# Two transformer blocks on one core: the last MLP's up product with seven block products per pair of feature tiles

## The reference

```python
h = _rmsnorm_2(x, mlp_norm_w[layer])
x = x + jnp.square(jax.nn.relu(h @ w_up[layer])) @ w_down[layer]
```

## Time and profile before

| | us |
|---|---|
| median of 3 runs | 3357.95 |
| lowest and highest | 3356.92, 3360.74 |
| span of the profiled execution | 3358.0 |
| its own busy time: PE, DVE, POOL, ACT | 3155.6, 1537.2, 1206.1, 816.2 |
| output product 2538 to 2643, last MLP 2643 to 3358 | 105, 715 |

### The profile page before, as it was taken

How to read it: one execution, slowest core, us unless ns; L and a number is a source line. 1 busy time by engine, 2 the same in 40 slices (tenths; PEclk the granted TensorE clock), 3 DMA queues, 4 the chain that set the end, 5 groups by cost and what they waited for, 6 DMA issues and landing times.

```text
span 3358.0 us, 34815 instructions
## 1 busy us (share of the span) xinstructions
PE 3155.6 (94%) x13555; PEld 2467.7 (73%) x13566; DVE 1537.2 (46%) x2220; ACT 816.2 (24%) x1186; POOL 1206.1 (36%) x567
## 2 busy tenths in 40 slices
PE   7999998999878799999999799889998999999999
PEld 5787775678656588888887477568666788888887
DVE  3799956553643621221122621255884532232236
ACT  3312215511224301000001332245774100000000
POOL 2254342334722244344333133173002344444443
PEclk9899999999989999999999899999999999999999
DMA  2022310034110011111111122442421111111111
GB/s 103 26 88 100 139 44 7 1 138 150 63 38 19 25 49 46 50 50 44 50 50 44 40 75 100 123 150 69 106 76 72 44 45 50 50 50 44 50 50 75
DMA packets 69272, 217.54 MB, mean 65 GB/s; under 512 B 7468, under 2 KB 18900, under 8 KB 68408
## 3 DMA queue, kind: packets, MB, share of 16 engines
q1 hardware_dynamic: 40832, 145.51, 14.0%
q10 hardware_dynamic: 28344, 70.74, 5.7%
HBM read 175.31 MB, written 40.65 MB: 64 GB/s over the span
## 4 chain that ended last, share of the span: by engine, by line
PE 87%; DVE 6%; ACT 4%; issue 1%; POOL 1%; ACTq 0%; DMA 0%; POOLq 0%; DVEq 0%
PE ps L519 25%; PE ps L521 25%; PE ps L520 25%; PE ps L557 3%; PE ps L720 2%; DVE y L1672 1%; PE ps L1036 1%; PE ps L1024 1%; DVE x L1673 1%; PE ps L710 1%; PE ps L1009 1%; POOL w_lo L419 1%; PE ps L1010 1%; DVE acc L1649 0%; POOL w_hi L416 0%
## 5 line engine op out<-in xcount | busy, mean ns | idle before, releaser
L416 POOL TENSOR_TENSOR w_hi<-w_raw,zero 128x1024 fp32r<-128x1024 f32 x210 | 407.5, 1940 | 1808.9 <-PE ps L521 1801.9
L519 PE MATMUL ps<-normed_hi,w_hi 128*128 128x512 f32 x1488 | 588.8, 396 | 34.7 <-DVE normed_lo L1657 18.2
L520 PE MATMUL ps<-normed_lo,w_hi 128*128 128x512 f32 x1488 | 583.7, 392 | 0.0
L521 PE MATMUL ps<-normed_hi,w_lo 128*128 128x512 f32 x1488 | 583.6, 392 | 0.0
L419 POOL TENSOR_TENSOR w_lo<-w_raw,w_hi 128x1024 fp32r<-128x1024 f32 x210 | 564.4, 2687 | 16.5
L519 PEld LDWEIGHTS ps<-normed_hi,w_hi 128*128 128x128 f32 x1488 | 282.5, 190 | 100.3 <-issue 28.6
L519 PE MATMUL ps<-hidden_hi,w_hi 128*128 128x512 f32 x864 | 336.9, 390 | 2.8 <-DVE hidden_lo L1888 2.8
L521 PE MATMUL ps<-hidden_hi,w_lo 128*128 128x512 f32 x864 | 336.8, 390 | 0.0
L520 PE MATMUL ps<-hidden_lo,w_hi 128*128 128x512 f32 x864 | 336.6, 390 | 0.0
L520 PEld LDWEIGHTS ps<-normed_lo,w_hi 128*128 128x128 f32 x1488 | 282.5, 190 | 60.8 <-issue 2.2
L521 PEld LDWEIGHTS ps<-normed_hi,w_lo 128*128 128x128 f32 x1488 | 282.2, 190 | 59.4
(11 more groups left out here) (360 smaller groups left out, 5179.9 us busy)
## 6 DMA issues: line engine op xcount, KB each, us to landing
w_raw<-weights_dram SPq DMA_DIRECT2D x228, 512.0 KB, 3.7
gates_scratch<-tmp ACTq DMA_DIRECT2D x24, 512.0 KB, 2.7
gated<-gates_scratch ACTq DMA_DIRECT2D x24, 512.0 KB, 5.4
head_part<-diff_qk_scratch SPq DMA_DIRECT2D x48, 256.0 KB, 6.4
x_in<-x_dram ACTq DMA_DIRECT2D x4, 1024.0 KB, 11.1
x<-x_dram ACTq DMA_DIRECT2D x1, 4096.0 KB, 13.9
diff_qk_scratch<-d_hi ACTq DMA_DIRECT2D x8, 512.0 KB, 2.7
diff_qk_scratch<-d_out ACTq DMA_DIRECT2D x8, 512.0 KB, 2.7
```

The source lines that it names most:

```text
L416: nc.gpsimd.tensor_tensor(w_hi[s][:], raw[s][:], zero[:, 0:1].broadcast_to([P, 1024]), ALU.add).then_inc(w_rounded, 1)
L519: nc.tensor.matmul(out, sh, mh, start=start, stop=False)
L520: nc.tensor.matmul(out, sh, ml, start=False, stop=False)
L521: return nc.tensor.matmul(out, sl, mh, start=False, stop=stop)
```

## The change

The 4096 features of the last MLP are taken in PAIRS = 16 pairs of tiles. The up product of a pair is seen as a 2 x 2 by 2 x 2 block product: the left side is weights (2 feature tiles by 2 halves of 4 input tiles), the right side x (2 halves of the input tiles by 2 halves of the tokens). A scheme of Strassen's kind (seven products, with sums ahead and behind) takes the place of eight block products. One block product is 4 x 3 = 12 matmuls into one PSUM bank.

- The sums of the right side (t1 to t4, minus_b22) are made once, and split (`right`, 7 pairs of 4 x 512 columns), by ACT and DVE; they fill the place of x, normed and hidden. So x goes to DRAM (`x_kept`) tile by tile from ACT's queue, is scaled in place, and comes back as `x_back` in the last pair from SP's queue.
- The sums of the left side are made by POOL per pair from four 128 x 512 parts. The high part is now rounded by ACT (`left_hi`), the remainder made by POOL (`left_rest`), with 4 buffers of 512 columns, used in turn. Per pair there are 11 of these: products 0 to 4, four for down, products 9 and 10. A22 is loaded a second time.
- Behind the products, ACT copies the first, and DVE forms the four quarters of the pair in 7 steps (`u_read`, `v_read`, `c12_read`, `c22_read` with two, `c11_read`, `c21_read`; they count in `post_done`); ACT takes relu, square and rounding (`hidden_part`), DVE the remainder (`hidden_rest`).
- The order on PE for pair c: products 0 to 4, the down product of pair c - 1 (8 tiles of 12 matmuls, two PSUM slots in turn), products 9 and 10. After the loop the down product of the last pair follows.
- Down results are added to `y_2`, in the place of x; the clearing of it waits for all of the right side. For output tiles 4 to 7 y_2 times acc goes to x_back one pair early, and the last pair's result is then multiplied from PSUM.

The diff, cut to its core ("..." where lines are left out; of the removed lines only the loop's; the DVE steps, `hidden_part` and the packing of the weights are told above):

```diff
-PRE_ORDER = ("mix_pre", "mem_pre", "ffn_pre", "attn_2", "q_a", "kv_a", "mlp_2")
+PRE_ORDER = ("mix_pre", "mem_pre", "ffn_pre", "attn_2", "q_a", "kv_a")
...
+PAIRS = FF2_TILES // 2
+LEFT = 11
+A11, A21, A22, A12, DOWN = 0, 1, 2, 3, 4
+A22_AGAIN = DOWN
+RAW_OF_LEFT = (A11, A22, A11, A11, A21, DOWN, DOWN + 1, DOWN + 2, DOWN + 3, A12, A22_AGAIN)
+BY_FIRST, BY_DOWN, BY_PLAIN = range(5), range(5, 9), (9, 10)
...
+        left = [(at(f"left_hi{i}", SPLIT + 4 * KB * i, [P, HALF], F32R),
+                 at(f"left_lo{i}", SPLIT + 4 * KB * i + 2 * KB, [P, HALF], F32R)) for i in range(4)]
+        part_at = [RAW + 2 * KB * i for i in range(4)] + [late_at + 2 * KB * i for i in range(4)]
+        part_in = [at(f"part_in{i}", o, [P, HALF]) for i, o in enumerate(part_at)]
+        right = {name: pair("right_" + name, o, [P, 4, HALF]) for name, o in (
+            ("b11", BR), ("t1", BR + 16 * KB), ("t2", BR + 32 * KB), ("minus_b22", BR + 48 * KB),
+            ("t3", AR), ("b21", AR + 16 * KB), ("t4", AR + 32 * KB))}
...
+        y_2 = at("y_2", XR, [P, KT, S])
+        x_back = at("x_back", BR, [P, KT, S])
...
+            def load_left(c, before, last=False):
+                first = isinstance(c, int) and c == 1
+                if not last:
+                    for i, used in ((A22, 2), (A11, 3), (A21, 4)):
+                        sp.wait_ge(w_split, before(used))
+                        load_part(i, c)
+                if first:
+                    sp.wait_ge(right_lo, right_0 + 28)
+                else:
+                    sp.wait_ge(w_split, before(5))
+                    load_again(c - 1)
+                if last:
+                    sp.wait_ge(w_used, left_at(PAIRS - 1, 1))
+                    for k in range(KT):
+                        sp.dma_start(x_back[:, k, :], t["x_kept"][k]).then_inc(x_back_in, 16)
+                for i in range(1, 4):
+                    sp.wait_ge(w_split, before(5 + i))
+                    load_part(DOWN + i, c - 1)
+                if not last:
+                    sp.wait_ge(w_split, before(9))
+                    load_part(A12, c)
+                sp.wait_ge(w_split, before(10))
+                load_part(DOWN, c - 1)
...
+            def left_rest(c, i):
+                hi, lo = left[i % 4]
+                pool.wait_ge(w_rounded, left_at(c, i))
+                tt(lo[:], part_in[RAW_OF_LEFT[i]][:], hi[:].bitcast(F32), ALU.subtract).then_inc(w_split, 1)
+            def split_pair(c, down=True):
+                pool.wait_ge(pair_landed, 48 * c + landed_0 + 48)
+                add_part(A22, A21, 1)
+                pool.wait_ge(left_summed, 4 * c + summed_0 + 1)
+                add_part(A21, A11, 2)
+                left_rest(c, 0)
+                pool.wait_ge(left_summed, 4 * c + summed_0 + 2)
+                pool.wait_ge(w_split, left_at(c, 0))
+                add_part(A11, A22, 3)
+                left_rest(c, 1)
+                left_rest(c, 2)
+                pool.wait_ge(late_landed, 16 * c + landed_0 + 16)
+                pool.wait_ge(w_split, left_at(c, 2))
+                add_part(A11, A12, 4)
+                for i in (3, 4, 5, 6, 7, 8, 9, 10) if down else (3, 4, 9, 10):
+                    left_rest(c, i)
...
+            def left_product(c, i, bank, name, ready=None):
+                hi, lo = left[i % 4]
+                pe.wait_ge(w_split, left_at(c, i))
+                for k in range(4):
+                    if ready:
+                        pe.wait_ge(right_lo, right_0 + ready[k])
+                    last = product(ps[:, bank, :], (hi[:, k * P:k * P + P], lo[:, k * P:k * P + P]),
+                                   tuple(v[:, k, :] for v in right[name]), k == 0, k == 3)
+                last.then_inc(w_used, 1)
+            def pair_first(c):
+                first = isinstance(c, int) and c == 0
+                pe.wait_ge(*((x_added, 3 * KT + 5) if first else (post_done, 7 * c + post_0 - 2)))
+                left_product(c, 0, 0, "b11", (7,) * 4 if first else None)
+                pe.wait_ge(*((x_added, 3 * KT + 6) if first else (post_done, 7 * c + post_0 - 1)))
+                left_product(c, 1, 2, "t1", (8,) * 4 if first else None)
+                if not first:
+                    pe.wait_ge(post_done, 7 * c + post_0)
+                left_product(c, 2, 1, "t2", (14, 14, 14, 16) if first else None)
+                if first:
+                    pe.wait_ge(x_added, 4 * KT)
+                left_product(c, 3, 7, "minus_b22", (15,) * 4 if first else None)
+                pe.wait_ge(first_copied, c + copied_0 + 1)
+                left_product(c, 4, 0, "t3", range(17, 21) if first else None)
...
+                pe.wait_ge(post_done, 7 * c + post_0 + 2)
+                left_product(c, 9, 2, "b21", range(21, 25) if first else None)
+                left_product(c, 10, 1, "t4", range(25, 29) if first else None)
...
+                pe.wait_ge(u_lo, 4 * c)
+                for m in range(KT):
+                    hi, lo = left[(5 + m // 2) % 4]
+                    if m % 2 == 0:
+                        pe.wait_ge(w_split, left_at(c, 5 + m // 2))
+                    pe.wait_ge(u_added, 8 * c + m - 1)
+                    for k in range(2):
+                        b = (m % 2 * 2 + k) * P
+                        for n in range(0, S, HALF):
+                            last = product(down_slot(m)[:, n:n + HALF], (hi[:, b:b + P], lo[:, b:b + P]),
+                                           tuple(v[:, k, n:n + HALF] for v in hidden_2), k == 0, k == 1)
+                    last.then_inc(w_used if m % 2 else first_half, 1)
...
-            mlp_chunk(0, 2)
-            with pe.Fori(1, FF2_TILES // CHUNK) as c:
-                mlp_chunk(c)
+            over_features(wide(2), acc, ones[:]).then_inc(n_sum, 1)
+            pair_last(0)
+            pe.wait_ge(n_rs, 10)
+            with pe.Fori(1, PAIRS) as c:
+                pair_first(c)
+                down_2(c)
+                pair_last(c)
+            down_2(PAIRS)
...
+            for k in range(KT - 1):
                 act.wait_ge(x_added, 3 * KT + k + 1)
+                act.dma_start(t["x_kept"][k], x[:, k, :]).then_inc(x_kept, 16)
                 post_square(3, k, x[:, k, :])
+                act.wait_ge(x_kept, kept_0 + 16 * k + 16)
+                act.wait_ge(n_post_sq, 3 * KT + k + 1)
+                nc.scalar.activation(x[:, k, :], x[:, k, :], ACT.Copy, scale=col("mlp_2", k)).then_inc(right_scaled, 1)
+                act.wait_ge(right_scaled, scaled_0 + k + 1)
+                if k < 4:
+                    right_round("b11", k, x[:, k, n1])
+                    act.wait_ge(right_formed, right_0 + k + 1)
+                    right_round("t1", k, t1_plain[:, k, :])
+                else:
+                    right_round("minus_b22", k - 4, x[:, k, n2], -1.0)
+                    act.wait_ge(right_formed, right_0 + k + 1)
+                    right_round("t2", k - 4, x[:, k - 4, n1])
+            left_hi(0, 0)
+            left_hi(0, 1)
+            left_hi(0, 2)
+            act.wait_ge(x_added, 4 * KT)
+            act.dma_start(t["x_kept"][KT - 1], x[:, KT - 1, :]).then_inc(x_kept, 16)
+            nc.scalar.activation(last_scaled[:], x[:, KT - 1, :], ACT.Copy, scale=col("mlp_2", KT - 1)).then_inc(right_scaled, 1)
+            act.wait_ge(right_scaled, scaled_0 + KT)
+            right_round("minus_b22", 3, last_scaled[:, n2], -1.0)
+            act.wait_ge(right_formed, right_0 + KT)
+            right_round("t2", 3, x[:, 3, n1])
...
+            copy_first(0)
+            left_hi(0, 3)
+            left_hi(0, 4)
+            for j in range(4):
+                right_round("t3", j, x[:, j, n2])
+            left_hi(0, 9)
+            post_square(3, KT - 1, x[:, KT - 1, :])
+            for j in range(4):
+                right_round("b21", j, x[:, 4 + j, n1] if j < 3 else last_scaled[:, n1])
+            left_hi(0, 10)
+            for j in range(4):
+                act.wait_ge(right_formed, right_0 + KT + j + 1)
+                right_round("t4", j, t4_plain[:, j, :])
...
+            with act.Fori(1, PAIRS) as c:
+                left_hi(c, 0)
+                hidden_c12(c - 1)
+                left_hi(c, 1)
+                hidden_c11(c - 1)
+                left_hi(c, 2)
+                hidden_c22(c - 1)
+                hidden_c21(c - 1)
+                copy_first(c)
+                for i in range(3, LEFT):
+                    left_hi(c, i)
+            hidden_c12(PAIRS - 1)
+            left_hi(PAIRS, 5)
+            hidden_c11(PAIRS - 1)
+            left_hi(PAIRS, 6)
+            hidden_c22(PAIRS - 1)
+            left_hi(PAIRS, 7)
+            hidden_c21(PAIRS - 1)
+            left_hi(PAIRS, 8)
...
+            def right_sums(j, second):
+                dve.wait_ge(right_scaled, scaled_0 + 5 + j)
+                dve.wait_ge(right_lo, right_0 + 8)
+                step(tt(x[:, j, n2], x[:, j, n2], second[:, n2], ALU.subtract))
```

(95 more changed lines are left out.)

215 lines of the change are left out of this document (139 added, 76 removed).

## The result

| | before | after |
|---|---|---|
| median, us | 3358.1 | 3335.0 |
| lowest and highest | 3356.9, 3360.7 | 3332.2, 3342.1 |
| span of the profiled execution | 3358.0 | 3340.3 (its time 3342.1) |

Both medians are of four runs. The ratio is 0.9935 (95% interval 0.9923 to 0.9948): 23 us, or 0.65%, faster, where 26 were predicted. The forecast's own case came in; 3335.0 lies 3.0 above its 3332.0.

What follows compares the result with a forecast made beforehand. TensorE matmuls were taken to bound the kernel. MLP start 2642.65, pair 0 and total 20.4 + 5.5, 15 pairs 612.3, clear 8, wait 10, last down 30, store 3.1: 3332 us after rounding, range 3318 to 3348.

Steps and rivals of the forecast that it cites:

- Removed matmuls, 43.5 us: Last MLP: 84 up matmuls per feature pair, not 96; 192 fewer at 0.2267 us save 43.5 us.
- Steady loop 0: Loop over pairs: added ACT, DVE and POOL work stays covered, costing 0 beyond matmuls; left 3 has 1.1 us to spare.
- Pair 0, 5.5 us: MLP entry: DVE's queue of sums and remainders makes product 10 end late, costing 5.5 us (4 to 12).
- Clear, 8 us: Pair 1: DVE's 6.9 us clear of y_2 ahead of c11_read delays products 1 to 3, costing 8 us (5 to 12).
- Wait before the last down product, 10 us: After the last pair's product 10, PE waits for hidden, made serially by ACT and DVE: 10 us (6 to 13).
- Last down product 30 us: Last down product to its last sum: DVE's three operations on tiles 0 to 3 hold up PE; 30 us.
- The round trip, 0: Return of x as x_back: its 4 MB load is covered, costing 0, at most 5 us.
- 1 (cheaper transitions): Transitions: DVE at its fast rows, no low clock, end wait 7, giving 3319 us; chance 0.12.
- 2: Loop: left 3 late in every pair by 0.3 to 1 us at full clock, 3336 to 3347 us; chance 0.15.
- 3: Loop: left 3's chain over 2 us late and the clock falls in each pair, 3388 us, slower; chance 0.06.
- 4, a clock that falls at the joins alone: Joins between 12-matmul groups: one clock fall a pair of 1.7 to 2.8 us, 3359 to 3377 us; chance 0.04.
- 5: Whole MLP: the change does not do what it says, matmuls stay at 3072, 3375 us; chance 0.01.

Runs made afterwards that it cites:

- eight-product kernel: Changed kernel with the t3 product made twice per pair, so as many matmuls as before the change: 3376.0 us, ratio 1.0058 to the kernel before.
- kernels with more copies: Changed kernel with one, three or six more 0.66 us ACT copies ahead of left_hi 3 each turn: 3331.4, 3351.0 and 3392.7 us.
- second execution: Changed kernel run once more, nothing altered: 3333.8 us, ratio 0.993 to the kernel before.
- fourfold edit: Changed kernel without y_2's clear, entry square sum earlier, last products 9 and 10 before the previous down product, end sums on POOL: 3317.0 us, ratio 0.9877.

## Why the prediction was right, and where it was off

- **Removed matmuls, 43.5 us:** right in price and number. The eight-product kernel gives those of 15 pairs back to 0.1 us; the 2.7 of pair 0 are hidden by its wait, so they are part of what the pair 0 term below measures. The Trainium skill's 216 ns (TensorE: Matmul & The Clock Gate, Back-to-back issue gap) would make these 38.9 for 40.9 measured; the trace's 0.2267 decided. The same section calls this the gap of isolated matmuls and gives about 131 ns for a stream of weight loads and matmuls in turn, as this kernel has; the measured 226.7 agrees with neither.
- **Steady loop 0:** right, and for the reason given: 1.1 us to spare were worked out, 1.2 are in the trace (0.8 to 0.9 by the kernels with more copies), and one more ACT step is free there where three are not.
- **Start of the MLP without a gap:** right. There is no wait at T0.
- **Pair 0, 5.5 us:** the mis-sized term. Measured 30.3 - 20.4 = 9.9. Of it the wait for the total is 6.4, low clock in and behind the total's matmuls 2.4, and a stop before product 3 is 0.8. DVE late with the last square sum was named, but as a wait of 1.7 us: the sum was put at 2658, 15.4 from T0, and ended at 20.8. Of these 5.4 us, 1.35 are DVE idle for ACT's rounding of t3, a wait that the step did not have; 1.4 are the t3 remainders (4.9 for 3.5) and 2.6 the t4 sums (5.6 for 3). Half-width operations were taken at 0.7 to 0.8 us, the fast rows, also where DVE and POOL worked at the same time; there they took 1.75 to 1.79. The rows of the kernel before already had the sign: 2.80 against 1.22 for one sum. The remainders of t4, which the step had as the last to hold PE up, were ready in time at 28.3. The step should have counted a DVE operation beside a POOL operation as waiting for it: 0.6 + 1.29 = 1.9 us by that rule, 1.7 measured from start to start.
- **Clear, 8 us:** right, 8.2 by the difference of the parts (660.7 - 30.3 - 9.9 - 612.3) and 7.3 to 7.8 by the kernel without it.
- **Wait before the last down product, 10 us:** right, 9.9. Taking it away brings only 6.9, since DVE's backlog of multiplications and sums, which that wait had hidden, then holds up PE itself (waits on y of 5.8 us in all, not 1.8).
- **Last down product 30 us:** 28.7, and 29.8 in the second execution, with DVE without idle time from its first eviction on, as said. The round trip, 0: right. The last store, 3.1: 3.0.
- **Rivals:** 1 (cheaper transitions) did not come by itself; the fourfold edit shows that it was to be had. 2 and 3 are about 1 us of ACT time away. 4, a clock that falls at the joins alone, is refuted for this kernel: 12-matmul groups on changing PSUM slots run five windows of 100 us at clock 1.00. The Trainium skill's rule in A second HAM failure mode: psum-queue depth-cycling (same page as above) speaks of short idle times between groups, and here there are none. 5 is refuted by the count of matmuls and by the eight-product kernel.

The sum was off by 4.4 - 1.3 - 0.1 = 3.0 us, so a second miss covered part of the first. The signs that the prediction's last paragraph names all came in.

## What to carry to other kernels

A kernel that is bound by matmuls in its loop gains the full price of each matmul removed there, as long as the sums that replace them lie on engines with time to spare at the tightest join. One removed where PE waits anyway gains nothing. The loss then sits in the transitions, so list there what each engine has to do in its order, and count an overlapping two-SBUF-input DVE operation and a POOL operation as one after the other. Before moving work from DVE to POOL, ask whether the two would meet on SBUF; an eviction from PSUM kept its 1.21 us.
